# First attention of a two-block transformer kernel: ScalarE writes out the differential heads' values product and its sum of squares

## The reference, cut to what matters

```python
p = jax.nn.softmax(s, axis=-1)
a = p[:, 0] - lam_full * p[:, 1]
o = jnp.einsum('bhqk,bkhd->bqhd', a.astype(v.dtype), v)
o = rms_norm(o, sub_norm.reshape(DIFF_HEADS, DIFF_V)) * (1.0 - lam_init)
```

## Time and profile before

| what | value |
|---|---|
| median of the runs | 3150.83 us (3150.15 to 3158.27) |
| the profiled execution's own time | 3151.19 us |
| its span from the first to the last instruction | 3149.5 us |
| TensorE matmuls busy | 98% of the span |
| TensorE weight loads | 77% |
| VectorE | 41% |
| ScalarE | 25% |
| GpSimd | 43% |
| mean granted TensorE clock | 0.984 |
| first attention, layer 0 | about 66 to 271 us |
| first attention, layer 1 | about 742 to 940 us |

### The profile page before, as it was taken

One profiled execution on the slowest core, in us unless ns is written; L12 is line 12 of the kernel. 1 busy time (PEld: TensorE's weight loads), 2 busy tenths in 40 slices (PEclk: granted clock), 3 DMA queues, 4 the chain that ended last, 5 costly groups with the idle time before them and its releaser, 6 DMA issues.

```text
span 3149.5 us, 40217 instructions
## 1 busy us (share of the span) xinstructions
PE 3071.1 (98%) x13996; PEld 2412.1 (77%) x13996; DVE 1276.8 (41%) x2913; ACT 801.5 (25%) x1799; POOL 1363.8 (43%) x924
## 2 busy tenths in 40 slices
PE   7999999999999999999999999999999999999998
PEld 6777788887777888887666868888676667688885
DVE  4484535344674433445614531111536226311123
ACT  2354212122362211213333131100223332300012
POOL 4222555554214555553223645555342235455552
PEclk9898999999999999999999999999999999999999
DMA  7322566665315666663233646666442236565662
GB/s 246 94 91 84 181 193 193 194 199 162 94 58 159 186 201 193 192 203 108 91 97 114 215 147 199 197 194 193 139 148 92 90 108 196 157 195 190 186 203 92
DMA packets 136517, 494.06 MB, mean 157 GB/s; under 512 B 15280, under 2 KB 15536, under 8 KB 136112
## 3 DMA queue, kind: packets, MB, share of 16 engines
q0 software_dynamic: 66240, 241.20, 25.0%
q1 hardware_dynamic: 68544, 245.40, 24.1%
q10 hardware_dynamic: 1584, 5.40, 0.5%
HBM read 489.84 MB, written 2.10 MB: 156 GB/s over the span
## 4 chain that ended last, share of the span: by engine, by line
PE 94%; DVE 2%; ACT 1%; issue 1%; DMA 1%; POOL 0%; ACTq 0%; POOLq 0%; DVEq 0%
PE ps L514 26%; PE ps L515 24%; PE ps L516 24%; PE ps L745 3%; PE ps L770 3%; PE ps L692 3%; PE ps L715 2%; PE ps L641 1%; PE ps L643 1%; PE ps L642 1%; PE ps L705 1%; PE ps L758 1%; PE ps L911 1%; PE ps L939 0%; PE ps L780 0%
## 5 line engine op out<-in xcount | busy, mean ns | idle before, releaser
L514 PE MATMUL ps<-hi,w_hi 128*128 128x512 f32 x3216 | 1287.5, 400 | 13.9 <-DVE lo L1043 7.5
L515 PE MATMUL ps<-hi,w_lo 128*128 128x512 f32 x3216 | 1261.2, 392 | 0.0
L516 PE MATMUL ps<-lo,w_hi 128*128 128x512 f32 x3216 | 1260.3, 392 | 0.0
L487 POOL TENSOR_TENSOR w_lo<-w_raw,w_hi 128x1024 fp32r<-128x1024 f32 x460 | 1106.7, 2406 | 97.2 <-DMA w_hi<-weights 87.6
L482 POOL DMA_DIRECT2D w_hi<-weights x460 | 261.1, 568 | 1643.6 <-PE ps L516 1519.8
L514 PEld LDWEIGHTS ps<-hi,w_hi 128*128 128x128 f32 x3216 | 608.2, 189 | 219.2 <-issue 77.3
L516 PEld LDWEIGHTS ps<-lo,w_hi 128*128 128x128 f32 x3216 | 608.5, 189 | 130.1
L515 PEld LDWEIGHTS ps<-hi,w_lo 128*128 128x128 f32 x3216 | 609.0, 189 | 118.9 <-issue 0.2
L1133 DVE CUSTOM_DVE_ANT_0 pr<-ps,kc 128x128 f32<-128x128 f32 (+2 forms) x160 | 65.3, 408 | 323.0 <-PE ps L745 323.0
L1820 ACT ACTIVATE ps<-hb,col 128x512 f32<-128x512 f32 x88 | 68.6, 782 | 381.2 <-DVE hb L1072 381.2
L1555 DVE SCALAR_TENSOR_TENSOR x<-x,ps 128x512 f32<-128x512 f32 x64 | 43.9, 688 | 287.1 <-PE ps L516 287.1
(11 more groups left out here) (316 smaller groups left out, 3133.6 us busy)
## 6 DMA issues: line engine op xcount, KB each, us to landing
w_raw<-weights SPq DMA_DIRECT2D x460, 512.0 KB, 3.5
w_hi<-weights POOLq DMA_DIRECT2D x460, 512.0 KB, 3.8
x<-xt SPq DMA_DIRECT2D x8, 256.0 KB, 10.3
out<-x SPq DMA_DIRECT2D x8, 256.0 KB, 2.0
kc<-k ACTq DMA_DIRECT2D x1, 1281.0 KB, 5.6
bias<-relb ACTq DMA_DIRECT2D x2, 512.0 KB, 5.1
bias<-relb ACTq DMA_DIRECT2D x1, 1024.0 KB, 5.1
praw<-pt ACTq DMA_DIRECT2D x2, 512.0 KB, 3.5
```

The lines of the kernel that those rows point to most:

```text
L487: nc.gpsimd.tensor_tensor(wlo[s][:, :], raw[s][:, :], whi[s][:, :].bitcast(F32), ALU.subtract).then_inc(w_split, 1)
L514: nc.tensor.matmul(out_ap, w[0], xx[0], start=first, stop=False)
L515: nc.tensor.matmul(out_ap, w[1], xx[0], start=False, stop=False)
L516: return nc.tensor.matmul(out_ap, w[0], xx[1], start=False, stop=last)
```

## The change

ScalarE takes over the writing out of the 48 differential tasks. In its pass `it`, ahead of its `side(it)`, it waits for the values product of task it-3, copies it out with the reciprocal as its scale, and squares it with the same scale into unused columns of the same bank, with the sum in the accumulator. A new semaphore `od_ready` counts these; `on_ready` counts the 40 tasks of the other kinds. VectorE skips L1107 and L1114 for differential tasks and keeps everything else. The transposes wait for the semaphore of the kind that last used the bank. The square already has the reciprocal twice, so `AT_FACTOR` multiplies 24 columns and not 48. The diff, cut to its core:

```diff
+        od_ready = sem("od_ready")
+        for kind in ("diff", "norm"):
+            for e, t in enumerate(t for l in range(L) for t in TASKS["1", l] if t.kind == kind):
+                t.more["e"] = e + 1
 ...
 TensorE, attention_1 and turn_chunk
-                            pe.wait_ge(on_ready, on0 + i - 2)
+                            pe.wait_ge(od_ready if ts[i - 3].kind == "diff" else on_ready, ts[i - 3].more["e"])
-                    pe.wait_ge(on_ready, q.on)
+                    pe.wait_ge(od_ready, 24 * (l + 1))
+                    pe.wait_ge(on_ready, 40 * (l + 1))
 ...
 VectorE, attention_1
-                    if 0 <= it - 4 < n:
+                    own = 0 <= it - 4 < n and ts[it - 4].kind == "norm"
+                    if own:
                         i, t = it - 4, ts[it - 4]
                         dve.wait_ge(pv_done, t.id + 1)
                         dve.wait_ge(rinv_ready, on0 + i + 1)
 ...
-                    if 0 <= it - 4 < n:
-                        if on0 + it - 4:
-                            dve.wait_ge(on_ready, on0 + it - 4)
+                    if own:
+                        if ts[i].more["e"] > 1:
+                            dve.wait_ge(on_ready, ts[i].more["e"] - 1)
 ...
 VectorE, AT_FACTOR
-                        dve.wait_ge(on_ready, q.on + 56)
-                        link(V.tensor_tensor(ss[:, 0:48], ss[:, 0:48], rinvs[:, 0:48], ALU.mult))
+                        dve.wait_ge(od_ready, 24 * (l + 1))
+                        dve.wait_ge(on_ready, 40 * l + 32)
+                        link(V.tensor_tensor(ss[:, 24:48], ss[:, 24:48], rinvs[:, 24:48], ALU.mult))
 ...
 ScalarE, attention_1, between the copy of the transposes and side(it)
+                    if 0 <= it - 3 < n and ts[it - 3].kind == "diff":
+                        i, t = it - 3, ts[it - 3]
+                        act.wait_ge(pv_done, t.id + 1)
+                        act.wait_ge(rinv_ready, on0 + i + 1)
+                        o_ap, k = ps[:, TO_BANK[i % 3], 0:64], t.more["ss"]
+                        A_(t.more["out"], o_ap, ACT.Copy, scale=rinv(k))
+                        if t.more["e"] > 1:
+                            act.wait_ge(od_ready, t.more["e"] - 1)
+                        A_(ps[:, TO_BANK[i % 3], 64:128], o_ap, ACT.Square, scale=rinv(k),
+                           accum_out=ss[:, k:k + 1]).then_inc(od_ready, 1)
                     side(it)
```

More of the change, by code:

```diff
@@ L718, in attention_1, with turn_chunk @@
                 q.on += n
-            def turn_chunk(src, c):
+            def turn_chunk(l, src, c):
                 if c < len(C_BANK):
-                    pe.wait_ge(on_ready, q.on)
+                    pe.wait_ge(od_ready, 24 * (l + 1))
+                    pe.wait_ge(on_ready, 40 * (l + 1))
                 else:
@@ L849, in _ @@
                 for c, src in enumerate(dn + mn):
-                    turn_chunk(src, c)
+                    turn_chunk(l, src, c)
                 def turn_last():
@@ L854, in turn_last @@
                     for c in range(2):
-                        turn_chunk(cn[c], 6 + c)
+                        turn_chunk(l, cn[c], 6 + c)
                     q.chunk += NC_
@@ L1372, in low_turned @@
                     q.chunk += 1
-                dve.wait_ge(on_ready, q.on)
+                dve.wait_ge(on_ready, 40 * (l + 1))
                 link(V.tensor_tensor(ss[:, 48:64], ss[:, 48:64], rinvs[:, 48:64], ALU.mult))
@@ L1649, in attention_1 @@
                 n = len(ts)
+                on0 = q.on
                 for it in range(n + 3):
@@ L1664, in attention_1 @@
                         A_(slots(i)[1][t.id % 2][:, 0:t.n], ps[:, TO_BANK[i % 3], 0:t.n], ACT.Copy).then_inc(pt_ready, 1)
+                    if 0 <= it - 3 < n and ts[it - 3].kind == "diff":
[8 more added lines that the diff above has]
+                           accum_out=ss[:, k:k + 1]).then_inc(od_ready, 1)
                     side(it)
+                q.on += n
             def attention(ts, slots, side=None):
```

## The result

The changed kernel takes 3161.05 us (median of 8 runs, 3156.19 to 3172.06), the kernel before, run beside it on the same chip, 3150.55 us (8 runs, 3142.85 to 3158.27). The ratio is 1.0036 [1.0023, 1.005], so 11 us later, between 7 and 16. A second measurement gave 3159.71 us (8 runs) against 3151.36 (29 runs), 1.0026 [1.0011, 1.0041]. The kernel is slower by the intervals of both. The size lies about at the bound of 0.3% (9.45 us) that the prediction set: the first measurement, by its median and by its ratio, is beyond it, the second within it. The profiled execution took 3160.49 us, its span is 3158.8 us, 9.3 more than before.

What follows compares the result with a forecast made beforehand. TensorE's matmuls, busy 98% of the span, bound the kernel; helpers count only where TensorE waits. Steps accumulating to 2.33 us in each of two layers gave 4.7 us on the median: 3155.5 us, range 3147.5 to 3162, no clock drop counted.

Steps and rivals of the forecast that it cites:

- V0: Small-tile stretch, pass 27: TensorE starts this tile 1.15 us later, as ScalarE waits 0.69 and works 0.46 before K0's copies.
- Q3: Pass 30 tile, needing V1's copy: two more evictions and 0.05 us of waiting bring the lateness to 2.12 us.
- Q5: Pass 33 tile, needing K1's copies: VectorE's gain takes 0.55 off, an eviction adds 0.46 + 0.1; lateness 2.13 us.
- V3: Pass 36 tile, needing K2's copies: the last eviction adds 0.2, lateness 2.33 us a layer, which then stays.
- the wait: ScalarE, ahead of its side work, waits for TensorE's values product of task it-3: 0.69 us before K0's copies.
- the pair: ScalarE's added copy and square of 64 columns with accumulator read, for each differential task: 0.46 us, bounds 0.24 and 0.75.
- the cover of the 12-matmul passes: Passes 16 to 23: ScalarE has 3 us to spare, hiding its added wait and work; these passes keep their length.
- the relief: VectorE freed of evictions: small-tile stretch gains at most 0.85 us a layer, 0.3 ahead of Q2 and 0.55 at Q4.
- e: ScalarE's cost of writing out one differential task: taken as 0.46 us, bounded between 0.24 and 0.75 us.
- rival 2: Passes 26 to 33: ScalarE becomes the bound and TensorE's clock falls; 3161.8 us, chance 0.09.
- Rival 1: Small-tile stretch: ScalarE has room, VectorE's freed time decides, 0.85 us a layer come back; 3149.1 us, chance 0.20.
- Rival 3: ScalarE: Square outside Exp's table brings two loads of 1.283 us per task; 3187 us or more, chance 0.01.

Runs made afterwards that it cites:

- `wait_only`: Kernel before, VectorE writing out all tasks, plus only ScalarE's wait for the values product of task it-3; 3157.84 us, ratio 1.0024 to the kernel before.
- `only_early`: Changed kernel, but ScalarE writes out only tasks 0 to 7 and 16 to 22, VectorE the others; 3151.83 us, ratio 0.9987 to the kernel before.
- the doubled pair: Changed kernel with a second Copy and Square on ScalarE for each differential task; 3179.33 us, ratio 1.0075 to the kernel before.
- `relief_only`: Kernel before, with nobody writing out the differential tasks, their outputs and sums of squares left out; 3149.19 us, ratio 0.9988 to the kernel before.
- `pass_later`: Changed kernel, but ScalarE writes out task it-4 in place of it-3, still ahead of its side work; 3152.89 us, ratio 1.0008 to the kernel before.

## Why the prediction was right, and what it mis-sized

**Right: the place and the four steps.** V0, Q3, Q5 and V3 were forecast at 1.15, 2.12, 2.13 and 2.33 us and measured at 1.17, 2.14, 2.20 and 2.36. The parts hold by themselves: the wait 0.68 us (forecast 0.69; `wait_only`), the pair 0.50 (0.46), the cover of the 12-matmul passes (`only_early`: under 0.1), the relief at Q4 (0.46 against 0.55). Start-to-start distances gave the pair. The Trainium skill, ScalarE: Activation LUTs, section Rules for kernel authors, gives an estimated 0.71 us for it; the trace disagrees, 0.50 us, and 0.99 for the doubled pair.

**Wrong in part: the relief.** At most 0.85 us a layer was 0.51 at best. The two places were right (0.31 us at Q2, 0.46 at Q4), adding them up was not: Q2's gain is lost at Q3, which waits for V1's copy on ScalarE. The sum didn't use it. The upper bound has a small slip too: at e = 0.75 the prediction's own steps give 3.29 us at Q5, not 3.39, so 7.6 us in all and not 7.8.

**Mis-sized: the clock.** The two layers' steps give 4.75 us (forecast 4.7), and the medians moved by 10.5 and 8.4. The prediction counted no drop in the sum and priced one at 1.57 us. That price came from a mean grant of 0.64 over one short stretch; a drop inside the small-tile passes cost 3.45 us, and the trace of before had stretches of 10.2 and 17.1 us at half clock from which a larger price could have been estimated. Over all 16 executions the changed kernel loses 55.7 us to the clock and not 52.0 (3.7 with a standard error of 1.6): 3.7 times 0.69 is 2.6 us. With 4.75 that is 7.3 of the 8.2 us by which the means differ. The last 0.9 is open; the means of the kernel before on the four chips lie up to 3.6 us apart.

**The range and the chances.** The range reached up to 3162 for the upper end of the pair's cost and one drop more in each layer. The time came to its upper part, 1 us under the end, by clock and not by e. So the waits were forecast by working, and that the median stayed inside the range is in part luck. Of rival 2 (ScalarE the bound and the clock falls) the second half occurred, without the first: a grant under 1.00 stood between 187 and 226 us, one of its marks, in one of two profiles (the other mark, a pair of 0.7 us, did not appear). With a drop priced at 3.45 us, one in each layer on top of 4.7 gives 11.6 us, beyond the bound of 9.45, with no need for e near its top. By that price the chance of "slower by over 0.3%" should have been well above 0.10.

**The rivals.** Rival 1 (the relief decides) falls with `relief_only`: there is 0.5 us a layer to win, and the wait costs more than that by itself. Rival 3 (table loads) falls with three loads before and after. The predicted indifference of passes 37 to 60 holds to 0.01 us.

**Open.** Why kernels so alike lose between 43 and 57 us to the clock. `wait_only` adds 1.4 us of waits and loses 5 to 6 us more than before, `pass_later` adds 4.0 and loses 5 less, both on one chip. It doesn't go by the number of stalls in this stretch, and no run took it apart.

## What to carry to other kernels

Work given to a half-idle engine costs by its place in that engine's program order: ahead of the copies that free a bank, a wait of 0.7 us and pairs of 0.5 us in nine passes became 2.4 us a layer; behind the copies, 0.6. Where a change of a few us is judged, follow one fixed instruction from profile to profile (layers and profiles of one kernel agreed within 0.06 us wherever the clock was full), and price a possible clock drop from the longer stretches that the old trace shows too, not from the shortest alone. And move only the few items that hold TensorE up: three tasks a layer shifted the transposes as much as freeing VectorE of all 24.

## What the runs showed of the hardware

**VectorE stands still while GpSimd subtracts.** A join (two tensor inputs in SBUF) of 512 columns takes 0.75 us alone. When GpSimd's fp32 subtraction of 2.4 us began 0.2 or 0.4 us after it, it took 3.15 and 3.35, while the subtraction kept its 2.4 us. The kernel before has eight joins in its first attentions that meet a subtraction. One of 256 columns (0.49 us alone), hidden by a 12-matmul pass:

```profile
847.48 2.51 DVE L1101 SCALAR_TENSOR_TENSOR mk<-mq,small,mk 128x256 f32<-128x256 f32 x1
```

```profile
847.30 2.38 POOL L487 TENSOR_TENSOR w_lo<-w_raw,w_hi 128x1024 fp32r<-128x1024 f32 x1
```

It began 0.18 us after the subtraction and ended 0.31 us after that one's end. Over all profiles this distance goes by the width alone: a join that meets a subtraction ends 0.16, 0.29, 0.43 and 0.56 us behind it for 128, 256, 384 and 512 columns, whether its row began 1.8 us after the subtraction's or up to 0.49 us before it. Each is 0.19 us less than the join takes alone. A join of 512 columns that began 0.70 us ahead got away whole (the changed kernel's, above). An estimate from the two head starts, 0.49 and 0.70 less 0.19: the subtraction holds VectorE's join from some 0.3 to 0.5 us ahead of its own row. A join-like instruction with one of its two tensors in PSUM was not held up: of the 176 at L1405 and L1407 of the kernel before, 166 overlap a subtraction, and none takes over 0.76 us, the same as alone. The Trainium skill, GPSIMD Engine Reference, section Key points, says that GpSimd shares its SBUF interfaces with VectorE and that instructions with two SBUF inputs contend. The trace agrees for two SBUF inputs, and shows that it is no slowing but a standstill.

**The cost of half clock is in its length.** The drops of these kernels are stretches at 0.50 of 3.4 to 20.5 us, in part in different places in two executions of one kernel (the changed kernel has one at 197.7 in one profile and none in the other). An execution gets longer by 0.69 us for each us so lost. That it is not the whole may come from TensorE's waits for others within the stretches; this is not shown.
